# Differential attention whose two score softmaxes are computed together on the two row halves of TensorE, in a hybrid transformer block on one Trainium2 core

## The reference, cut to what matters

```python
def diff_attention(q, k, v, lam):
    s = jnp.einsum('bqhtd,bmhtd->bhtqm', q, k).astype(jnp.float32) * DIFF_DIM ** -0.5
    p = jax.nn.softmax(s, axis=-1)
    a = p[:, :, 0] - lam * p[:, :, 1]
    return jnp.einsum('bhqm,bmhe->bqhe', a.astype(v.dtype), v)

def diff_out(o, norm_g, lam_init):
    b, n, h, d = o.shape
    return (rmsnorm(o, norm_g) * (1.0 - lam_init)).reshape(b, n, h * d)
```

## Time and profile before

| | us |
|---|---|
| three runs | 2715.16, 2712.33, 2713.06, median 2713.06 |
| the profiled execution, its own time | 2720.91 |
| its span in the trace | 2719.1 |
| PE matmul busy | 2434.4 (90% of the span) |
| DVE busy | 908.9 (33%) |
| ACT busy | 544.8 (20%) |

### The profile page before, as it was taken

How to read it: one execution, slowest core, us unless ns; L and a number is a source line. 1 busy time by engine, 2 the same in 40 slices (tenths; PEclk the granted TensorE clock), 3 DMA queues, 4 the chain that set the end, 5 groups by cost and what they waited for, 6 DMA issues and landing times. The chain is left out here.

```text
span 2719.1 us, 37721 instructions
## 1 busy us (share of the span) xinstructions
PE 2434.4 (90%) x16456; PEld 1660.6 (61%) x16456; DVE 908.9 (33%) x1769; ACT 544.8 (20%) x1284; POOL 222.8 (8%) x269
## 2 busy tenths in 40 slices
PE   4999989969975999999999999897676599999998
PEld 2656655548874855555569998455422385444698
DVE  2124712267751422222220022326655623222111
ACT  2102631242202311111110021114411022111110
POOL 1000000027740000000000000000011200000000
PEclk8898989989997999999999999998887799999999
DMA  8251001000012101011025556110100011121354
GB/s 299 95 184 31 1 23 40 0 1 4 4 31 96 62 31 62 31 62 62 31 60 162 168 177 212 62 62 16 59 0 0 0 62 62 62 93 62 87 149 138
DMA packets 190786, 193.46 MB, mean 71 GB/s; under 512 B 4970, under 2 KB 174622, under 8 KB 190430
## 3 DMA queue, kind: packets, MB, share of 16 engines
q1 hardware_dynamic: 177950, 145.55, 17.6%
q0 software_dynamic: 11584, 42.24, 4.3%
q10 hardware_dynamic: 1088, 3.26, 0.3%
HBM read 188.94 MB, written 2.10 MB: 70 GB/s over the span
## 5 line engine op out<-in xcount | busy, mean ns | idle before, releaser
L1402 PE MATMUL banks<-mem 128*128 128x512 f32 x1312 | 618.1, 591 | 0.0
L1736 PE MATMUL banks<-mem 128*128 128x128 f32 x3520 | 405.4, 277 | 11.2 <-PEq L1325 9.9
L1736 PEld LDWEIGHTS banks<-mem 128*128 128x128 f32 x3520 | 400.7, 194 | 21.2 <-issue 19.8
L461 DVE SCALAR_TENSOR_TENSOR mem<-banks,mem 128x511 f32<-128x511 f32 (+1 forms) x168 | 106.0, 660 | 750.3 <-ACT mem L1473 327.0
L1402 PEld LDWEIGHTS banks<-mem 128*128 128x128 f32 x1312 | 247.8, 189 | 171.9 <-issue 153.2
L1405 PEld LDWEIGHTS banks<-mem 128*128 128x128 f32 x672 | 127.1, 189 | 162.0 <-issue 162.0
L1405 PE MATMUL banks<-mem 128*128 128x256 f32 x672 | 200.1, 378 | 0.0
L1821 PE MATMUL banks<-mem 128*128 128x512 f32 x400 | 192.9, 614 | 5.3 <-issue 5.3
L1471 ACT ACTIVATE mem<-banks,mem 128x512 f32<-128x512 f32 x88 | 60.7, 690 | 629.9 <-PE banks L1405 373.5
L1347 PE MATMUL banks<-mem 128*128 128x256 f32 x640 | 144.8, 387 | 13.2 <-PEq L671 11.1
L873 PE MATMUL banks<-mem 64*64 64x64 f32 x3840 | 127.4, 220 | 18.5 <-DVE mem L1149 11.4
(11 more groups left out here) (307 smaller groups left out, 2743.3 us busy)
## 6 DMA issues: line engine op xcount, KB each, us to landing
mem<-in_ffn_w_up SPq DMA_DIRECT2D x44, 1024.0 KB, 5.4
mem<-in_ffn_w_down SPq DMA_DIRECT2D x64, 704.0 KB, 6.6
mem<-in_w_mod POOLq DMA_DIRECT2D x40, 1024.0 KB, 7.4
mem<-in_ab_w_in SPq DMA_DIRECT2D x14, 1024.0 KB, 5.5
mem<-in_w_mod SPq DMA_DIRECT2D x8, 1024.0 KB, 14.8
mem<-in_cd_w_in SPq DMA_DIRECT2D x8, 1024.0 KB, 5.7
mem<-in_ab_w_out SPq DMA_DIRECT2D x4, 1024.0 KB, 9.2
mem<-in_cd_w_out SPq DMA_DIRECT2D x4, 1024.0 KB, 5.1
```

Source lines behind the costliest of these rows:

```text
L461: step = v.scalar_tensor_tensor(out[:, 1:n], src[:, 0:n - 1], tap(0), out[:, 1:n], ALU.mult, ALU.add)
L1402: last = nc.tensor.matmul(c.ps[:, bank, :], w[:, k, :], ht[:, k, 0:N_X], start=k == 0, stop=k == KT - 1)
L1736: last = c.nc.tensor.matmul(c.ps[:, n % self.n_banks, 0:128], hidden[:, k, t * 128:(t + 1) * 128], w, start=k == 0, stop=k == FT - 1)
```

## The change

The stage is rewritten, with the same units in the same order:

- PE does both halves of a unit's scores one after the other, for the unit after the present one (two units are in flight in two sets of three PSUM banks). A unit's 1536 score columns lie without a gap in three banks, so the middle bank holds the end of softmax 0 and the beginning of softmax 1; the matmul into its first half waits for the one into its second half (`bank_shared`).
- PE's order in a step is scores, values, turn. ACT's is turned copy, both exponentials, keep. The values have one PSUM place instead of two, in the bank that also holds the end of `turn`, so a turn waits until the preceding unit's values are kept (`kept`), and the keep is the last thing in ACT's step.
- The weighing is one pass over the matrix: softmax 0 unnormalised plus softmax 1 times a ratio; the inverse sum of softmax 0 is applied in the keep, as a scale operand of 128x1.
- In the tail, the inverse RMS is Sqrt on ACT and a reciprocal on DVE.

```diff
@@ tensor @@
-            def scores(u, s):
+            def scores(u):
                 q, h, first = units[u]
-                if u:
-                    pe.wait_ge(exped, 2 * (u - 1) + s + 1)
-                r = slice(64 * s, 64 * s + 64)
...
+                if u >= 2:
+                    pe.wait_ge(exped, 2 * (u - 2) + 2)
+                cut = 1024 - N_ALL
+                parts = [(1, N_X, N_ALL), (0, N_X, N_ALL)] if first else \
+                    [(0, 0, N_X), (1, 0, cut), (1, cut, N_ALL), (0, N_X, N_ALL)]
+                for s, a, b in parts:
+                    r = slice(64 * s, 64 * s + 64)
+                    if (s, a, first) == (0, N_X, 0):
+                        pe.wait_ge(bank_shared, u + 1)
+                    last = nc.tensor.matmul(score(u, s)[:, a:b], qk[r, h, q * 128:(q + 1) * 128], qk[r, 4 + h, a:b],
+                                            start=True, stop=True)
...
             def turn_unit(u):
                 pe.wait_ge(weighed, u + 1)
                 if u:
-                    pe.wait_ge(turned_sb, u)
+                    pe.wait_ge(kept, u)
...
-            for i in range(n_units + 3):
-                if i < n_units:
-                    scores(i, 0)
-                if 0 <= i - 2 < n_units:
-                    turn_unit(i - 2)
-                if i < n_units:
-                    scores(i, 1)
-                if 0 <= i - 3 < n_units:
-                    values(i - 3)
+            scores(0)
+            for i in range(n_units + 2):
+                if i + 1 < n_units:
+                    scores(i + 1)
+                if 0 <= i - 2:
+                    values(i - 2)
+                if 0 <= i - 1 < n_units:
+                    turn_unit(i - 1)
@@ scalar @@
+            for i in range(n_units + 2):
+                if i >= 2:
+                    turned_copy(i - 2)
                 if i < n_units:
                     exps(i, 0)
...
                     exps(i, 1)
...
+                if i >= 2:
+                    keep(i - 2)
+            nc.scalar.activation(rstd, rstd, ACT.Sqrt, bias=EPS, scale=1.0 / 128).then_inc(rooted, 1)
@@ vector @@
-                    link(nc.vector.tensor_scalar(prob[:, u % 3, 1, first:N_ALL], prob[:, u % 3, 1, first:N_ALL],
-                                                 lam[:, b, 1:2], None, ALU.mult))
...
+                link(nc.vector.reciprocal(inverse[:, b, :], total[:, b, :]))
+                link(nc.vector.scalar_tensor_tensor(ratio[:, b:b + 1], inverse[:, b, 1:2], c.stat[:, 203:204],
+                                                    total[:, b, 0:1], ALU.mult, ALU.mult))
+                nc.vector.scalar_tensor_tensor(prob[:, u % 3, 0, first:N_ALL], prob[:, u % 3, 1, first:N_ALL],
+                                               ratio[:, b:b + 1], prob[:, u % 3, 0, first:N_ALL],
+                                               ALU.mult, ALU.add).then_inc(weighed, 1)
```

More of the change, by code:

```diff
@@ L492, in diff_attention @@
     by_unit = raw.rearrange("p k t -> p (k t)").rearrange("p (n e) -> p n e", e=128)
-    top, neg, total, lam = (c.stat[:, i * 4:i * 4 + 4].rearrange("p (b s) -> p b s", b=2) for i in range(4))
+    top, neg = (c.stat[:, i * 4:i * 4 + 4].rearrange("p (b s) -> p b s", b=2) for i in range(2))
+    total = c.stat[:, 64:72].rearrange("p (b s) -> p b s", s=2)
+    inverse = c.stat[:, 72:80].rearrange("p (b s) -> p b s", s=2)
+    ratio = c.stat[:, 80:84]
     rstd = c.stat[:, 16:16 + 4 * TT]
@@ L513, in _ @@
         def _(pe):
-            def scores(u, s):
+            def scores(u):
                 q, h, first = units[u]
-                if u:
-                    pe.wait_ge(exped, 2 * (u - 1) + s + 1)
-                r = slice(64 * s, 64 * s + 64)
[L519 to L523, removed]
+                if u >= 2:
[9 more added lines that the diff above has]
+                                            start=True, stop=True)
+                    if b == N_ALL:
+                        last.then_inc(scored[s], 1)
+                    elif s:
+                        last.then_inc(bank_shared, 1)
             def turn_unit(u):
@@ L568, in exps @@
                 first = units[u][2]
-                act.wait_ge(maxed, 2 * u + s + 1)
+                act.wait_ge(maxed, 2 * u + 2)
                 if u >= 3:
                     act.wait_ge(turned_ps, u - 2)
-                nc.scalar.activation(prob[:, u % 3, s, first:N_ALL], score(s)[:, first:N_ALL], ACT.Exp,
+                nc.scalar.activation(prob[:, u % 3, s, first:N_ALL], score(u, s)[:, first:N_ALL], ACT.Exp,
                                      bias=neg[:, u % 2, s:s + 1], scale=scale,
-                                     accum_out=total[:, u % 2, s:s + 1]).then_inc(exped, 1)
@@ L576, in _, with turned_copy, keep @@
-            for i in range(n_units + 4):
+                                     accum_out=total[:, u % 4, s:s + 1]).then_inc(exped, 1)
+            def turned_copy(u):
+                first = units[u][2]
+                act.wait_ge(turned_ps, u + 1)
+                nc.scalar.activation(turned[:, u % 2, first:N_ALL], turn[:, first:N_ALL], ACT.Copy).then_inc(turned_sb, 1)
+            def keep(u):
+                act.wait_ge(valued, u + 1)
+                nc.scalar.activation(by_unit[:, place(u), :], valued_at, ACT.Copy,
+                                     scale=inverse[:, u % 4, 0:1]).then_inc(kept, 1)
+                act.wait_ge(kept, u + 1)
+                link(nc.scalar.activation(junk, by_unit[:, place(u), :], ACT.Square,
+                                          accum_out=rstd[:, place(u):place(u) + 1]))
@@ L587, in _ @@
-                if i < n_units:
-                    exps(i, 1)
[L589 to L595, removed]
@@ L614, in maxima, with weigh @@
                                         ALU.mult).then_inc(maxed, 1)
[L616 to L625, removed]
-                    link(nc.vector.tensor_scalar(prob[:, u % 3, 1, first:N_ALL], prob[:, u % 3, 1, first:N_ALL],
-                                                 lam[:, b, 1:2], None, ALU.mult))
[L628 to L632, removed]
+            def weigh(u):
+                first = units[u][2]
+                b = u % 4
+                dve.wait_ge(exped, 2 * u + 2)
+                if u >= 4:
+                    dve.wait_ge(kept, u - 3)
+                link(nc.vector.reciprocal(inverse[:, b, :], total[:, b, :]))
[4 more added lines that the diff above has]
+                                               ALU.mult, ALU.add).then_inc(weighed, 1)
+            for i in range(-1, n_units + 1):
+                if 0 <= i - 1:
+                    weigh(i - 1)
+                if i + 1 < n_units:
+                    for s in range(2):
+                        maxima(i + 1, s)
             dve.wait_ge(rooted, 1)
+            link(nc.vector.reciprocal(rstd, rstd))
             for h in range(4):
```

21 lines of the change are left out of this document (10 added, 11 removed).

## The result

The changed kernel took 2697.95 us (median of five, 2695.71 to 2703.22) against 2714.1 for the kernel before on the same chips (2712.33 to 2718.59): ratio 0.9941, 95% interval 0.9926 to 0.9955. A second series gave 0.995 (0.9938 to 0.9962). So the gain is 13 to 16 us, within the range of 2688 to 2704, 2 to 5 us less than the 18 forecast. One execution of experiment 3 took 6413 us, in a slower state, and is left out of its ratio (though not of its median). The changed kernel's profiled execution took 2698.33 us, with a span of 2696.5.

What follows compares the result with a forecast made beforehand. The prediction took PE's queue to bound the latent units. Its terms, -10.9 - 0.7 - 3.2 - 1.3 - 2.5 + 1, summed to -17.6, taken as -18 off the median of 2713.1: 2695 us, range 2688 to 2704.

Steps and rivals of the forecast that it cites:

- twelve full cycles: Latent units: a cycle falls from 5.31 to 4.40 us, -10.9 us over twelve.
- units 14 and 15: Last latent units, with short scores ahead: 7.4 us together against 8.16 before, -0.7 us.
- context units, to the table load: Context units: 20.5 us in place of 23.7, cycle 2.2, -3.2 us, with +2 possible as no engine has slack.
- tail, load to scaling: Tail: one table load, with Sqrt and a DVE reciprocal of about 0.2 us, -1.3 us.
- start, to the end of turn 1: Head of the stage: between no gain at the half clock and -5.7 us at full clock, taken as -2.5.
- end, at the clock: Last context units and tail: the half clock may come earlier relative to the work, 0 to +3, taken as +1 us.
- Scores, the overlap: Latent scores on PE: both halves run at once on different row halves, 1.53 us in place of 2.98.
- Rival 2: Scores on PE: no overlap of the halves, scores 2.93, cycle 5.8, 2721 us, slower; chance 0.05.
- Scores, the shared bank: Latent scores: the wait for the other half's 256 columns ends about 0.7 us in, covered by 0.2 us.
- Rival 1: Scores on PE: overlap in program order only, segment 1.89 us in place of 1.53, 2701 us; chance 0.12.
- Round trip through the keep: Values to turn: handover 0.04, keep 0.37 with scale operand, back to PE 0.05; PE waits about 0.5 us a cycle.
- ACT and DVE keep up: Latent cycle of 4.40 us: ACT ready half a microsecond early, DVE needs 3.5; removing L626 is hidden.

Runs made afterwards that it cites:

- experiment 3: The changed kernel with the 256 shared-bank columns of softmax 1 ahead of the 512 columns of softmax 0 in the scores; 2692.49 us, ratio 0.9914.
- experiment 6: The changed kernel with softmax 1 also on partitions 0 to 63, so no overlap of the row halves (another result, same work); 2728.15 us, ratio 1.0056.
- experiment 7: The changed kernel with the weighing as two DVE passes again, multiply then add; 2704.4 us, ratio 0.9954.
- experiment 8: The two-pass weighing on the kernel of experiment 5; 2693.95 us, ratio 0.9918.
- experiment 9: The kernel of experiment 5 with the context units' turn in a bank without the values, needing no wait for the keep; 2686.14 us, ratio 0.9891.
- experiment 4: The changed kernel with the turn waiting for the keep only ahead of its fifth block; 2694.24 us, ratio 0.9927.
- experiment 5: The changed kernel with both edits, the scores' short part first and the turn waiting only at its fifth block; 2689.51 us, ratio 0.9912.

## Why the prediction was right, and where it was not

The terms of the sum against the first pair of profiles, each as the prediction counted it:

| term | forecast | measured |
|---|---|---|
| twelve full cycles | -10.9 | 57.0 - 63.7 = -6.7 |
| units 14 and 15 | -0.7 | 7.92 - 8.16 = -0.24 |
| context units, to the table load | -3.2 | 22.8 - 23.75 = -0.95 |
| tail, load to scaling | -1.3 | 1.89 - 3.09 = -1.2 |
| start, to the end of turn 1 | -2.5 | 15.0 - 18.0 = -3.0 |
| end, at the clock | +1 | -0.45 |
| stage | -17.6 | -12.5 |

By the signs that the prediction named, the idle before the turn (0.55 us, put down to the keep) and the single table load stand for it; the scores segment, 1.82 us, stands nearer to its sign of being wrong (1.9) than to the 1.5 it gave.

- **What bounds the kernel**: right. PE's queue was the bound, and taking work off it shortened the stage; a kernel without the overlap is slower than before (experiment 6).
- **Scores, the overlap**: right in mechanism. The trace of unit 0 was the decisive reading; in every cycle the loads and passes of both halves run side by side. Rival 2 is what experiment 6 built, and it ended slower, with a cycle of 5.71 where 5.8 was worked out, and 2728 where 2721 was; the excess is not in the cycle.
- **Scores, the shared bank**: this is the step that failed. The prediction said "The wait is covered by 0.2 us", counting from the end of the awaited pass on its own row half. The semaphore came only with the end of the long pass ahead of it in program order, 0.45 us after the awaited pass. It cost 1.82 - 1.49 = 0.33 us in each latent unit, 4 us in twelve, which is most of the 5.1 us that the stage lacks, and experiment 3 gives it back by changing the order of two matmuls. Rival 1, overlap in program order, gave 1.89 for the segment and 2701, close to the 1.82 and to the measured 2698 to 2701, but by another mechanism: the starts are not in program order (six loads within 0.73 us of the segment's start; in experiment 3 eight in one run), only the signals are.
- **The rule on program order**: the Trainium skill, page "TensorE: Matmul & The Clock Gate", section "The mechanism", says that matmuls both start and end in program order. The traces here don't agree on starts across row halves: in the changed kernel the second long pass of softmax 0 starts 0.2 us after the awaited pass of softmax 1, which stands behind it in the program. Nor do the modelled ends (286.23 and 285.80). What does follow program order is the semaphore (experiment 3).
- **Round trip through the keep**: right in mechanism and nearly in size: 0.55 us of waiting against 0.5; the handover back to PE was 0.11 and not 0.05. The 0.04 for the handover to ACT held, though not for the reason given: the reduction in the earlier trace rows waits for softmax 0 alone, whose last pass ends 0.04 us before the end shown there. The scale operand cost the estimated 0.10: the keep takes 0.37.
- **ACT and DVE keep up**: right (experiment 7), and the removed pass L626 is worth nothing in this kernel.
- **Units 14, 15 and the first context unit**: mis-sized, 3.96, 3.96 and 3.53 us against 3.9, 3.5 and 3.1. The scores ahead take 0.67, but the values can't start before the turned copy is done, 1.03 us in; I checked the keep against ACT and not the copy.
- **Context units**: the full cycle was right (2.23 against 2.2). The three at the end took 331.5 to 339.6, 8.1 us against the 6.4 of the sum, because the half clock came at 333.3, ahead of the last two. The term "end +1" stood for this; with the 0.45 gained in the row "end" it measured +1.3, so it was sized nearly right, and most of what the row "context units" lacks belongs to it. ACT's lack of slack, for which the prediction held +2 to be possible, cost no more than 0.1 us in five cycles.
- **Tail and start**: right. To the end of turn 1 it is 15.0 and 14.3 us in the two profiles of the changed kernel, 18.0 and 17.5 in those of the kernel before. How much of this is the shorter half clock (3.3 and 3.4 us against 13.6 and 10.1) and how much the other order of work was not separated.

So the forecast of 2695 was near by some luck: the stage gave 12.5 in place of 17.6, and the first series' median lay 16 below. The measured 2698 and 2701 lie at least as near to the 2701 of the first rival as to the forecast. The second series, 13 below, and the second profiles (122.8 against 111.45, 11.4) are nearer to what the stage shows.

## What to carry to other kernels

- Two matmuls on different row halves ran at once here even though they stand behind one another in the queue (1.49 us for both halves of the scores in experiment 3, as for one alone in the earlier trace rows), but don't count on a semaphore of one of them before everything ahead of it in program order has ended (0.45 us here). Put the matmul that somebody waits for first.
- Where a wait guards a PSUM bank, put it ahead of the first instruction that writes that bank and not ahead of the group; here this alone was worth nearly as much as the change's own saving in a cycle (0.49 against 0.56 us).
- A pass that is taken off an engine that isn't the bound is worth nothing until the others are fast enough; measure it again then (0.0 us a cycle in experiment 7, 0.17 in experiment 8).

## What the runs showed of the hardware that was not expected

- The order of signals, above: awaited pass over at 0.70 us, its semaphore rises at 1.15, its waiter starts at 1.20; with the order of two matmuls changed (experiment 3) the semaphore rises 0.01 us after the awaited pass.
- The half clock (a granted clock of 0.50) at the head of the stage lasted 13.6, 10.1 and 27.2 us in three profiles of the kernel before (the third with the new tail) and 23.8 in experiment 6, so in all kernels without the overlap. With the overlap it lasted 3.3 and 3.4 us in the changed kernel, 3.4 in experiment 9, 10 in two pieces in experiment 7, and does not appear in experiments 3, 4, 5 and 8. Whether the overlap is the reason isn't shown. PE was busy for 27.02 of the 27.2 us before the clock rose; why it lasted so long stays open. With 27.2 in place of 13.6 us of it the stage was 6 us longer (129.38 with the 1.2 us of the tail added, against 124.44): this is larger than the effects of half of the experiments and is why their cycles, and not their medians, decide.
- A 128x24 reciprocal on DVE took 0.30 us where I had taken 0.2.
